# Branch B of a gated attention block: another order of the next pair's tiles, the rotation cut into six operations, two transposes in other banks

## What is computed

```python
def mla_attention(q_nope, q_rope, k_nope, k_rope, v):
    # queries in 4 blocks of 128; keys of later chunks of 64 are masked
    scale = (B_NOPE + B_ROPE) ** -0.5
    ...
        s = (jnp.einsum('bqhd,bkhd->bhqk', qn, k_nope)
             + jnp.einsum('bqhd,bkd->bhqk', qr, k_rope)).astype(jnp.float32) * scale
        s = jnp.where(allowed[None, None], s, MASK_VALUE)
        p = jax.nn.softmax(s, axis=-1)
        return jnp.einsum('bhqk,bkhd->bqhd', p.astype(v.dtype), v)
...
qb_rope = apply_rope(qb[..., B_NOPE:], cos_b, sin_b)
out_b = mla_attention(qb_nope, qb_rope, kb_nope, kb_rope, vb) * jax.nn.silu(b_g)
```

## Time and profile before

| | us |
|---|---|
| median of 3 runs | 716.95 (716.85 to 717.15) |
| the profiled execution | 716.98 |
| span of its trace, first to last instruction | 715.0 |
| TensorE busy | 683.7 |
| GpSimd, VectorE, ScalarE busy | 321.6, 316.6, 303.2 |
| branch B, from the first S0 to the last product | about 423 to 555 |

### The profile page before, as it was taken

How to read it: one execution, slowest core, us unless ns; L and a number is a source line. 1 busy time by engine, 2 the same in 40 slices (tenths; PEclk the granted TensorE clock), 3 DMA queues, 4 the chain that set the end, 5 groups by cost and what they waited for, 6 DMA issues and landing times.

```text
span 715.0 us, 9017 instructions
## 1 busy us (share of the span) xinstructions
PE 683.7 (96%) x3282; PEld 567.6 (79%) x3282; DVE 316.6 (44%) x515; ACT 303.2 (42%) x573; POOL 321.6 (45%) x150
## 2 busy tenths in 40 slices
PE   5999999999979999999999997999999999999995
PEld 4888887888858888888888786878778888888884
DVE  6957120980693553543443576776852110100013
ACT  6722232212124564564464475566653141322233
POOL 3654443444433233433443335545675275464630
PEclk9999999999999999999999999999999999999999
DMA  8632222333221122212322312210121932232215
GB/s 286 218 125 98 103 88 89 89 97 110 88 88 61 60 89 89 88 60 89 96 81 89 119 59 89 89 61 29 60 60 60 352 119 89 88 117 88 89 48 217
DMA packets 21588, 73.47 MB, mean 103 GB/s; under 512 B 2352, under 2 KB 2480, under 8 KB 21424
## 3 DMA queue, kind: packets, MB, share of 16 engines
q1 hardware_dynamic: 18144, 66.07, 27.2%
q10 hardware_dynamic: 3408, 6.90, 2.7%
HBM read 68.77 MB, written 4.19 MB: 102 GB/s over the span
## 4 chain that ended last, share of the span: by engine, by line
issue 40%; PE 32%; POOL 18%; DVE 5%; ACT 3%; DMA 1%; POOLq 0%; SPq 0%; DVEq 0%; ACTq 0%
POOL w_lo L244 18%; PE bank L946 10%; PE bank L950 10%; PE bank L949 10%; DVE t L811 1%; DVE pb L852 1%; PE bank L1142 1%; DVE st_b L844 1%; DMA xs<-x_t 1%; DVE ptb_lo L857 1%; ACT pb L475 1%; PE bank L1132 0%; PE bank L1133 0%; DMA w_raw<-w_stream 0%; ACT x_hi L323 0%
## 5 line engine op out<-in xcount | busy, mean ns | idle before, releaser
L244 POOL TENSOR_TENSOR w_lo<-w_raw,w_hi 128x1024 fp32r<-128x1024 f32 x109 | 266.4, 2448 | 324.3 <-ACT w_hi L317 323.7
L946 PE MATMUL bank<-x_hi,w_hi 128*128 128x512 f32 x520 | 204.9, 394 | 2.9 <-DVE t L631 2.9
L317 ACT ACTIVATE w_hi<-w_raw 128x1024 fp32r<-128x1024 f32 x110 | 116.1, 1058 | 210.0 <-PE bank L946 190.7
L950 PE MATMUL bank<-x_lo,w_hi 128*128 128x512 f32 x520 | 202.9, 390 | 0.0
L949 PE MATMUL bank<-x_hi,w_lo 128*128 128x512 f32 x520 | 202.5, 389 | 0.0
L946 PEld LDWEIGHTS bank<-x_hi,w_hi 128*128 128x128 f32 x520 | 97.8, 188 | 23.3 <-DVE t L631 3.3
L950 PEld LDWEIGHTS bank<-x_lo,w_hi 128*128 128x128 f32 x520 | 97.6, 188 | 20.7
L949 PEld LDWEIGHTS bank<-x_hi,w_lo 128*128 128x128 f32 x520 | 97.7, 188 | 19.5 <-issue 0.5
L946 PE MATMUL bank<-w_hi,mx_hi 128*128 128x512 f32 x256 | 101.0, 394 | 0.0
L949 PE MATMUL bank<-w_hi,mx_lo 128*128 128x512 f32 x256 | 100.0, 391 | 0.0
L950 PE MATMUL bank<-w_lo,mx_hi 128*128 128x512 f32 x256 | 99.9, 390 | 0.0
(11 more groups left out here) (177 smaller groups left out, 911.1 us busy)
## 6 DMA issues: line engine op xcount, KB each, us to landing
w_raw<-w_stream SPq DMA_DIRECT2D x110, 512.0 KB, 3.3
xs<-x_t SPq DMA_DIRECT2D x8, 512.0 KB, 4.4
y<-x_nat ACTq DMA_DIRECT2D x4, 1024.0 KB, 9.1
out<-y SPq DMA_DIRECT2D x8, 512.0 KB, 3.6
fw<-final_w ACTq DMA_DIRECT2D x1, 1024.0 KB, 15.6
cos_b<-tables ACTq DMA_DIRECT2D x2, 256.0 KB, 2.7
sin_b<-tables ACTq DMA_DIRECT2D x2, 256.0 KB, 2.9
cos_r<-tables ACTq DMA_DIRECT2D x1, 256.0 KB, 3.5
```

The source lines that it names most:

```text
L244: pool.tensor_tensor(w_lo[:, s % HL, :], w_raw[:, s % RAW, :], w_hi[:, s % HL, :].bitcast(F32), ALU.subtract)\
L317: act.activation(w_hi[:, s % HL, :], w_raw[:, s % RAW, :], ACT.Copy).then_inc(w_hi_ready, 1)
L946: ins = pe.matmul(dst, ah, bh, start=start, stop=False)
L950: return pe.matmul(dst, ah, bl, start=False, stop=stop)
```

## The change

Four things, all in branch B:

1. The tiles of pairs 1 to 3 are projected in the order of pair 0: rotary queries, queries, keys, values (4, 5, 6, 0, 3, 1, 2), and the weight stream is laid out to match. `B_PIECES`, `B_SPLITS` and `B_CHUNKS` follow. TensorE's wait for `b_lo` at 6 moves from F0 to F2.
2. The rotation is six parts: the cosine product at F2, one sine product each at F3 and F4, two at F5, the sum at F6. Its split goes from F8 to F7 on ScalarE, ahead of tile 0's copies, and stays at F8 on VectorE.
3. T2 goes to bank 7 and T6 to bank 5. So T2 and T6 no longer wait for the low part before them, and T3 and T7 wait only for that of T1 and T5. T6 waits for S7's exponential instead, and the next pair's S1 for T6's low part.
4. `gate(3)` moves from VectorE to GpSimd, ahead of the low part of weight chunk PB0+5.

```diff
-B_PIECES = [((0, (0, 1)),), ((1, (0, 1)),), ((2, (0, 1)),), ((3, (0, 1)),), ((4, (0, 1)),), ((4, (2, 3)),), ((5, (0, 1)),),
-            ((5, (2, 3)),), ((6, (0, 1)),), ((6, (2, 3)),), ()]
-B_SPLITS = {1: 0, 2: 1, 3: 2, 4: 3, 8: 5, 10: 6}
-B_CHUNKS = {0: 0, 5: 1, 6: 2}
-B_ROTARY = {6: 0, 7: 1}
+B_PIECES = [((4, (0, 1)),), ((4, (2, 3)),), ((5, (0, 1)),), ((5, (2, 3)),), ((6, (0, 1)),), ((6, (2, 3)),), ((0, (0, 1)),),
+            ((3, (0, 1)),), ((1, (0, 1)),), ((2, (0, 1)),), ()]
+B_SPLITS = {4: 5, 6: 6, 7: 0, 8: 3, 9: 1, 10: 2}
+B_CHUNKS = {1: 0, 3: 1, 6: 2}
+B_ROTARY = {2: (0,), 3: (1,), 4: (2,), 5: (3, 4), 6: (5,)}
+B_ROTARY_HIGH, B_ROTARY_LOW = 7, 8
+T_BANK = (6, 6, 7, 6, 6, 6, 5, 6)
...
             def b_transpose(w):
                 pe.wait_ge(b_probs, w + 1)
-                pe.wait_ge(b_pt_lo, w + 1)
+                if T_BANK[w % 8] == 5:
+                    pe.wait_ge(b_exp, w + 4)
+                elif T_BANK[w % 8] == 7:
+                    pe.wait_ge(b_out, w // 4 + 1)
+                    pe.wait_ge(a_out, 17)
+                elif w > 0 and T_BANK[(w - 1) % 8] != 6:
+                    pe.wait_ge(b_pt_lo, w)
+                else:
+                    pe.wait_ge(b_pt_lo, w + 1)
...
             for c in range((b_head - 1) // HL * HL, b_head):
+                if c == b_head - 1:
+                    for ct in range(2):
+                        pool.wait_ge(gate_silu, 12 + ct + 1)
+                        pool.wait_ge(a_out, 12 + 5)
+                        pool.tensor_tensor(mixed[:, 6 + ct, :], mixed[:, 6 + ct, :], gate_tmp[:, ct, :], ALU.mult).then_inc(gated, 1)
                 low_part(c, c)
...
-                            if p == 0 and f == 0:
+                            if p == 0 and f == 2:
                                 pe.wait_ge(b_lo, 6)
...
-                    if p == 0 and step == "F" and f == 2:
-                        gate(3)
```

More of the change, by code:

```diff
@@ L270, in _ @@
                 low_part(c, c)
-            with pool.Fori(1, b_head // HL) as i:
+            with pool.Fori(1, (b_head - 1) // HL) as i:
                 for s in range(HL):
                     low_part(HL * i + s, s)
-            for c in range(b_head // HL * HL, b_head):
+            for c in range((b_head - 1) // HL * HL, b_head):
+                if c == b_head - 1:
[3 more added lines that the diff above has]
+                        pool.tensor_tensor(mixed[:, 6 + ct, :], mixed[:, 6 + ct, :], gate_tmp[:, ct, :], ALU.mult).then_inc(gated, 1)
                 low_part(c, c)
@@ L519, in _ @@
                     elif step[0] == "F":
-                        if p == 0 and f == 3:
+                        if p == 0 and f == 1:
                             act.wait_ge(gated, 8)
@@ L808, in b_rotary @@
                     dve.tensor_tensor(t1[:, :], bk[:, :], cos_b[own][:, :], ALU.mult)
[L809 to L812, removed]
+                elif part <= 4:
+                    q = part - 1
+                    o = q ^ 1
+                    ins = dve.tensor_tensor(t2[32 * q:32 * q + 32, :], bk[32 * o:32 * o + 32, :], sin_b[own][32 * q:32 * q + 32, :], ALU.mult)
+                    if part == 4:
+                        ins.then_inc(b_rot_evac, 1)
                 else:
@@ L863, in b_take @@
                 dve.tensor_tensor(m, B[7][:, :], m, ALU.mult).then_inc(b_out, 1)
-            for part in range(2):
+            for part in range(6):
                 b_rotary(0, part)
@@ L895, in _ @@
                         if p < PAIRS - 1:
-                            if f in B_ROTARY:
-                                b_rotary(p + 1, B_ROTARY[f])
-                            if f == 8:
+                            for part in B_ROTARY.get(f, ()):
+                                b_rotary(p + 1, part)
+                            if f == B_ROTARY_LOW:
                                 b_rotary_low(p + 1)
@@ L1126, in b_score @@
                 pe.wait_ge(b_exp, w + 1)
+                if w % 8 == 1 and w > 1:
+                    pe.wait_ge(b_pt_lo, w - 1)
                 if i == 0:
                     pe.wait_ge(b_rot_lo, w // 8 + 1)
-                    pe.wait_ge(b_lo, 3 + h if w < 8 else 6 * (w // 8) + 5 + h)
+                    pe.wait_ge(b_lo, 6 * (w // 8) + 3 + h)
                 dst = B[4 + w % 2][:, 0:n]
@@ L1173, in out_rows @@
                     ins.then_inc(o_done, 1)
-            for j in TILE_ORDER[0]:
+            for j in TILE_ORDER:
                 b_project(0, j, (0, 1) if j < 4 else (0, 1, 2, 3))
@@ L1258, in laid_out_weights @@
         parts = [np.concatenate([kn, v], axis=2), np.concatenate([qr, pad], axis=2), qn]
-        stream += parts[1:] + parts[:1] if p == 0 else parts
+        stream += parts[1:] + parts[:1]
     for n in range(4):
```

46 lines of the change are left out of this document (24 added, 22 removed).

## The result

The change makes the kernel slower, as forecast, but by nearly twice as much (9 us by the ratio, where 5 were forecast):

| us | before | after |
|---|---|---|
| median | 717.05 (716.85 to 717.94) | 726.77 (723.08 to 728.31) |
| ratio, with its 95% interval | | 1.0126 (1.0106 to 1.0145) |
| the profiled execution, its span | 716.98, 715.0 | 727.38, 725.1 |
| granted clock, mean of the span | 0.996 | 0.981 |

The account below looks back on a forecast made before the run. TensorE's stream bounds the kernel now; after, ScalarE and VectorE set pairs' ends. 716.98 + 0.2 (pair 0) + 3.0 + 3.2 (pairs 1, 2) - 1.3 (pair 3) = 722.1, said as 722.0; 8 in 10: 712 to 724.5.

Parts of the forecast that it names:

- point 2: Rotation's six parts on VectorE: S2's maximum to S6's takes 12.8 us, so S6's exponential starts 2.1 us late.
- Point 5: Pairs 1 and 2: 32.1 us against 29.1 (+3.0) and 33.15 against 30.0 (+3.2), ends set by ScalarE and VectorE.
- point 6: Pair 0, gate products on GpSimd: +1.1 if S0's normalising product loses to GpSimd, else -0.8; middle taken, +0.2 us.
- rival D: The forecast itself: slower, since S6's exponential to next S0 needs 11.1 us in series on ScalarE and VectorE; chance 0.56.
- point 3: ScalarE's queue behind S6: T5's high part starts 6.75 us after S6's exponential, 27.75 in the pair against 24.9 before.
- point 4: Pair's end: VectorE's two qr operations wait for GpSimd's low parts; S0 comes 4.35 us after T5's high part.
- Point 1: T2 and T6 in other banks end TensorE's waits there for the low part: -1.3 us in pair 3.
- A: VectorE and GpSimd do not contest SBUF at a pair's end: S0 2.35 us after T5's high part, 716.1 us; chance 0.22.
- B: VectorE's slip is absorbed in its 0.61 us gaps, S6's exponential about 1.3 us less late: 712.3 us; chance 0.12.
- C: TensorE stays the bound: all waits for low parts (9.5 us) and pair 0's lower clock (1.7) go, 705.8 us; chance 0.10.

Follow-up runs that it names:

- experiments 2 to 4: Variants of after: rotated queries split early, 716.43 us; GpSimd's low part held, 720.72; short subtractions, 724.72; rotation products directly after maxima, 722.39, or in one block, 719.14.
- the early split: After, with ScalarE's qr copies ahead of tile 6's and VectorE's subtractions ahead of T4's low part: 716.43 us, ratio 0.9991.
- the held low part: After, with GpSimd's low part of tile 3 held until VectorE has split the rotated queries: 720.72 us, ratio 1.0047.
- the rotation in a block: After, with all five rotation products in one block at F6 and the splits at F8: 719.14 us, ratio 1.0025.
- behind the maxima: After, with the five rotation products directly after the maxima of S2 to S6 instead of after the low parts: 722.39 us, ratio 1.0066.
- The late S0 in the kernel before: Kernel before, with one repeated 512 column VectorE subtraction at the end of pairs 0 to 2, for which S0 waits: 731.93 us, ratio 1.0209.
- experiment 1: Two kernels: the kernel before with one repeated VectorE subtraction that S0 waits for, 512 columns (731.93 us, ratio 1.0209) or 64 (726.05, ratio 1.0119).
- the best kernel found: After, with products after maxima, early query split, tile 6 copied at F5, pair 0's start altered, mixed output's first split at F0: 708.09 us, ratio 0.9863.

## Why the forecast was too low

**The step that failed: the forecast put the clock behind the new stops at nothing.** It foresaw a new stop of TensorE in front of each S0, but points 2 and 5 take the way from S0 to S2 at the full clock ("S2's maximum ... 7.5"), and its one remark on the clock, in point 6, is on pair 0: "TensorE has slack in either case". I had read the clock as a thing of pair 0. Behind each of after's stops at S0 the clock went to half. S2's maximum came at 10.05 instead of 7.5: 2.55 us that no term held. In the four kernels of experiments 2 to 4 where the clock stayed full behind pair 1's S0 it is at 7.23 (the early split, the held low part, the rotation in a block) and 7.50 (behind the maxima). The late S0 in the kernel before measured the same term by itself, 2.86 us from S0 to S4. TensorE had no slack there, since S0 to S2 is the part of a pair in which VectorE waits for TensorE (it is idle for 2.33 us at 461.23). A row could have warned: the pair with the longest wait, 3.7 us at T1, is the one with a clock below 1.00.

**The rest of the chain held**, and with it rival D's mechanism. Pair 1:

| | forecast | measured in after |
|---|---|---|
| S2's maximum, in the pair | 7.5 | 10.05 |
| S2's maximum to S6's (point 2) | 12.8 | 13.03 |
| S6's maximum to its exponential | 0.65 | 0.65 |
| from there to T5's high part (point 3) | 6.75 | 6.72 |
| from there to the next S0 (point 4) | 4.35 | 3.79 |
| pair 1 | 32.1 | 34.24 |

The held low part shows S6's exponential at 20.92 in the pair (475.99), where the forecast has 21.0. **Point 4** had the right mechanism, 0.56 us too large: the first subtraction waited 0.44 us where I put 0.7, the second 0.97 where I put 1.3. With the early split both are at 0.69. The Trainium skill's rule that I named there ("SBUF — State Buffer", Who interferes with whom) is borne out, and the order that it leaves open can be read from 486.58 to 490.07: GpSimd's `kn_lo`, VectorE's `qr`, `kn_lo`, `qr` in turn, with the held low part as the test of it.

**Point 5** gave pairs 1 and 2 +3.0 and +3.2; measured +5.15 and +5.13. In pair 2, 33.15 was forecast and 35.12 measured, of which the half clock took 2.65 (S0 to S4 14.19 us, 490.18 to 504.37, against 11.54 before).

**Point 6**, pair 0: +0.2 forecast, -0.1 measured. VectorE's products in after, to be read beside the earlier trace rows:

```profile
426.60 2.13 DVE L869 TENSOR_SCALAR pb<-pb,st_b 128x128 f32<-128x128 f32 x1
...
431.97 1.85 DVE L869 TENSOR_SCALAR pb<-pb,st_b 128x384 f32<-128x384 f32 x1
```

S0's product lost again, and so did S2's; for that case the forecast had +1.1. The -0.1 is luck in part: pair 0 itself is 0.6 us longer than before (33.42 against 32.84), but its S0 starts 0.65 sooner (422.52 against 423.17). No term held that, and it varies in kernels with the same work ahead of it (422.33 and 423.17 in the two of experiment 1).

**Point 1**, pair 3: -1.3 forecast, -0.1 measured. No wait for a low part is left in pair 3. But S0 to S4 is 14.41 us there (525.30 to 539.71) against 12.84, +1.57 for 3.4 us of half clock, which eats the gain. The term itself was right: in the kernel before with the new banks alone, 198.3 us pass from pair 3's S0 to the end, 1.6 less than before.

**The sum again:** 716.98 - 0.1 + 5.15 + 5.13 - 0.1 = 727.1, of the 727.38 measured. With full clock, each S0 to S4 as long as before (2.71, 2.65 and 1.57 less), it would be by my estimate 716.98 - 0.1 + 2.4 + 2.5 - 1.7 = 720.1, which is 2 us under the forecast and inside its range. After's executions spread over 5.2 us, where before has 1.1. Their mean clocks fit half clock that comes or doesn't as a part of it: 0.981 at 727.38 and 728.31 us, 0.988 at 723.08 and 726.17, some 10 us less of half clock (an estimate, 2 x 0.007 x 725). I have the trace of one of them only, so where it was missing is not shown, and the 3 us between the last two it doesn't explain.

**The rivals.** A fell: the lock was contested. B fell: S6's exponential was late by 2.05 us even where the clock stayed full (20.92 in the pair with the held low part, 18.87 before). C fell for this change; the best kernel found, 708.09, comes within 2.3 us of its 705.8. The Trainium skill's rule named with C ("Perfetto Trace Analysis", Optimizing Scalar/DVE Operations), that smaller instructions may let work end sooner, holds here only in the right place: the same five operations put S6's maximum 2.1 us later behind the low parts and no later behind the maxima.

## What to carry to other kernels

Where TensorE is nearly full, don't price a new wait by its length alone: look in the trace for a wait of that length, and read the granted clock and the matmul spacing behind it. Before an operation is moved in a queue, ask what is idle at the new place; a product behind a maximum filled idle time, and behind a low part it delayed the next maximum. Put what the next stage's first instruction needs where its inputs are first ready, not last, and keep it from the place where GpSimd works on SBUF.
